# Indexer scores of the sample tokens by pairs in four column groups, earlier stores of the chunk inputs, weight tiles between small products, top-k inside the chunks

## The reference

```python
def _indexer_scores(qi, wi, ki):                      # 8 index heads of 64
    logits = jnp.einsum('bthd,bsd->bths', qi, ki)
    return jnp.einsum('bths,bth->bts', jax.nn.relu(logits), wi)
...
# prompt: 256 keys per query, the 64 largest are kept; sample: 1024 + 4 keys, the 256 largest are kept
...
def step(S, inp):                                      # mixer B, 16 heads, state 64 x 64
    r_t, dec_t, k_t, v_t, a_t, b_t = inp
    sa = jnp.einsum('bhij,bhj->bhi', S, a_t)
    S = S * dec_t[:, :, None, :] + sa[..., None] * b_t[:, :, None, :] + v_t[..., None] * k_t[:, :, None, :]
    return S, jnp.einsum('bhij,bhj->bhi', S, r_t)
```

## Time and profile before

| | |
|---|---|
| median of 3 runs | 2201.64 us |
| the profiled execution | 2200.62 us |
| its span | 2198.8 us |
| TensorE busy | 2071.0 us, 94% |
| VectorE busy | 1053.5 us, 48% |
| ScalarE busy | 748.1 us, 34% |
| mean granted TensorE clock | 0.957 of full |

### The profile page before, as it was taken

How to read it: one execution, slowest core, us unless ns; L and a number is a source line. 1 busy time by engine, 2 the same in 40 slices (tenths; PEclk the granted TensorE clock), 3 DMA queues, 4 the chain that set the end, 5 groups by cost and what they waited for, 6 DMA issues and landing times.

```text
span 2198.8 us, 38331 instructions
## 1 busy us (share of the span) xinstructions
PE 2071.0 (94%) x15658; PEld 1850.0 (84%) x15658; DVE 1053.5 (48%) x1262; ACT 748.1 (34%) x1005; POOL 39.6 (2%) x60
## 2 busy tenths in 40 slices
PE   5999966999998999998999899999999999899997
PEld 4999754658885765557999899999999999899997
DVE  4444865806765620114444455554545554343434
ACT  3333302352223210004444345444444444233332
POOL 0000002100000000000000000000000000000000
PEclk9999987899998998888999999999999999999998
DMA  5444344234542289992454555444444444454543
GB/s 190 161 159 165 109 157 133 65 98 133 172 144 87 77 312 359 378 372 95 165 172 155 186 193 166 170 170 156 169 171 158 168 172 158 162 170 159 169 159 122
DMA packets 97260, 375.76 MB, mean 171 GB/s; under 512 B 28003, under 2 KB 38883, under 8 KB 69795
## 3 DMA queue, kind: packets, MB, share of 16 engines
q1 hardware_dynamic: 71058, 335.36, 43.7%
q10 hardware_dynamic: 21152, 19.66, 2.8%
q0 software_dynamic: 4976, 19.71, 2.6%
HBM read 358.14 MB, written 16.53 MB: 170 GB/s over the span
## 4 chain that ended last, share of the span: by engine, by line
PE 85%; DVE 7%; DMA 3%; SPq 2%; ACT 2%; issue 1%; DVEq 0%; ACTq 0%; POOL 0%; POOLq 0%
PE ps L425 13%; PE ps L921 13%; PE ps L922 13%; PE ps L923 12%; PE ps L876 5%; PE ps L877 5%; PE ps L878 5%; PE ps L460 2%; PE ps L459 2%; PE ps L461 2%; PE ps L817 2%; PE ps L849 1%; DMA gram<-arena 1%; PE ps L861 1%; PE ps L581 1%
## 5 line engine op out<-in xcount | busy, mean ns | idle before, releaser
L1776 DVE TENSOR_TENSOR weights_lo<-ring,weights_hi 128x2048 fp32r<-128x2048 f32 (+1 forms) x152 | 305.6, 2011 | 294.1 <-ACT weights_hi L1330 284.1
L922 PE MATMUL ps<-h_lo,weights_hi 128*128 128x288 f32 x1408 | 416.2, 296 | 0.0
L921 PE MATMUL ps<-h_hi,weights_hi 128*128 128x288 f32 x1408 | 414.6, 294 | 0.3 <-DVE weights_lo L1776 0.3
L923 PE MATMUL ps<-h_hi,weights_lo 128*128 128x288 f32 x1408 | 412.5, 293 | 0.0
L1330 ACT ACTIVATE weights_hi<-ring 128x2048 fp32r<-128x2048 f32 (+1 forms) x152 | 257.1, 1691 | 374.8 <-PE ps L923 365.7
L425 PE MATMUL ps<-hT,ring 128*128 128x288 f32 x1472 | 380.4, 411 | 1.2 <-ACT arena L1107 1.2
L425 PEld LDWEIGHTS ps<-hT,ring 128*128 128x128 f32 x1472 | 273.3, 191 | 79.4 <-issue 7.0
L923 PEld LDWEIGHTS ps<-h_hi,weights_lo 128*128 128x128 f32 x1408 | 265.1, 188 | 0.0
L921 PEld LDWEIGHTS ps<-h_hi,weights_hi 128*128 128x128 f32 x1408 | 264.1, 188 | 0.5 <-DVE weights_lo L1776 0.5
L922 PEld LDWEIGHTS ps<-h_lo,weights_hi 128*128 128x128 f32 x1408 | 264.4, 188 | 0.1
L921 PE MATMUL ps<-act_hi,weights_hi 128*128 128x288 f32 x704 | 209.7, 298 | 6.1 <-DVE weights_lo L1776 4.2
(11 more groups left out here) (339 smaller groups left out, 3083.3 us busy)
## 6 DMA issues: line engine op xcount, KB each, us to landing
ring<-in_wst SPq DMA_DIRECT2D x201, 1024.0 KB, 4.9
ring<-in_wdn SPq DMA_DIRECT2D x64, 704.0 KB, 4.0
arena<-in_kT SPq DMA_DIRECT2D x64, 512.0 KB, 5.7
arena<-in_v SPq DMA_DIRECT2D x64, 512.0 KB, 5.9
ring<-in_wst ACTq DMA_DIRECT2D x8, 1024.0 KB, 8.0
arena<-chunk_ar_bk ACTq DMA_DIRECT2D x24, 256.0 KB, 3.7
arena<-in_ki SPq DMA_DIRECT2D x64, 64.0 KB, 1.8
chunk_ar_bk<-arena POOLq DMA_DIRECT2D x2, 2048.0 KB, 14.4
```

What stands on the lines that cost most here:

```text
L921: mm(out, W_HI[:, (u - U_FF) % 2, w], hi, start=start, stop=False)
L922: mm(out, W_HI[:, (u - U_FF) % 2, w], lo, start=False, stop=False)
L923: return mm(out, W_LO[:, u % 4, w], hi, start=False, stop=stop)
L1776: tt(W_LO[:, u % 4, 0:m], raw, W_HI[:, at, 0:m].bitcast(F32), ALU.subtract).then_inc(sem("w_split"), 1)
```

## The change

- `scores(pair)` takes two sequences: four products of 32 rows, for two sequences and two halves of the 1024 keys, to the four groups of 32 columns of one bank. ScalarE applies one relu to all of it. `scores_sum(pair)` is two products, one for each half of the keys, which add into two banks over the four pairs (`start=(pair == 0)`, `stop=(pair == 3)`) with weights `WSM` that hold zeros for the other sequences. The scores of the new tokens with themselves are a small group of their own in bank 7. The sum of 32 rows goes straight to `SCS`, so the stores and the load of `sample_scores` go.
- All queries are built at once (`QS`), and three key buffers of two sequences each take the place of two of one sequence.
- GpSimd stores `ARt` when it is done, `BKt` in two halves, and loads the states; SyncE stores the grams.
- One tile stands between two grams, two between rotary products, one after every second prompt score product, and one between the groups of the 128 state products.
- Eight of the 16 prompt score products, those of the second query tile, move behind `sample_step(9)`, and the last step between them. 141 tiles are done where the chunks begin, 137 before.
- The prompt top-k goes into the chunks, one turn at the end of each; the mask `MP` is made after the last.

The diff, cut to its core:

```diff
@@ SyncE
             ki_pages(0)
-            ki_pages(1)
-            units(8, U_VKQ + 8, unit)
-            for b in range(NB):
...
+            units(8, U_VKQ + 7, unit)
+            for c in range(NCH):
+                sp.wait_ge(sem("gram_out"), c + 1)
+                sp.dma_start(gram_d[c], GS[:, c % 2, :]).then_inc(sem(f"gram_stored{c % 2}"), 16)
+            ki_pages(1)
+            units(U_VKQ + 7, U_VKQ + 8, unit)
+            ki_pages(2)
+            units(U_VKQ + 8, U_VKQ + 9, unit)
+            sp.wait_ge(sem("sidx"), 1)
+            ki_pages(3)
@@ TensorE
+            def scores(pair):
+
+                pe.wait_ge(sem(f"ki_in{pair % 3}"), 16 * 2 * NPG * (pair // 3 + 1))
+                if pair:
+                    pe.wait_ge(sem("sidx_relu"), pair)
+                for n in range(4):
+                    half, a = n // 2, n % 2
+                    ins = mm(ps[2][32 * n:32 * n + 32, :], QS[:, 2 * pair + a, :],
+                             KIB[pair % 3][:, a, half * 512:(half + 1) * 512], start=True, stop=True)
+                ins.then_inc(sem("sidx"), 1)
+
+            def scores_sum(pair):
+
+                pe.wait_ge(sem("sidx_relu"), pair + 1)
                 for half in range(2):
+                    at = 64 * half
+                    ins = mm(ps[3 + half][0:NSAMP, :], WSM[at:at + 64, pair, :], RL[at:at + 64, :],
+                             start=(pair == 0), stop=(pair == 3), skip_group_check=True)
+                ins.then_inc(sem("sidx_sum"), 1)
...
+            fill(U_VKQ, 75, 78)
+            scores_sum(0)
+            sample_step(0, 78)
+            fill(U_VKQ, 86, 89)
+            scores(1)
...
+            fill(U_VKQ, 110, 115)
+            sample_step(6)
+            fill(U_VKQ, 115, 121)
+            sample_step(7)
+            fill(U_VKQ, 121, 127)
+            sample_step(8)
+            fill(U_VKQ, 127, 133)
+            sample_step(9)
+            pe.wait_ge(sem("scs_out"), 2)
+            for n in range(IH, 2 * IH):
+                prompt_scores(n)
+                fill(U_VKQ, 125 + n, 126 + n)
+                if n == IH + 5:
+                    sample_step(10)
+            at_tile = 141
@@ VectorE
-            with dve.Fori(0, TOPK_P // 8) as i:
...
+            def prompt_largest():
+
                 for qt in range(2):
-                    settle(dve)
                     ch(nc.vector.max(out=M8[:, qt, :], in_=SCP[:, qt, :]))
...
                 if n < 4:
                     update(n)
                 largest()
+                prompt_largest()
@@ GpSimd
-            for a, src in enumerate((ARt, BKt)):
-                pool.dma_start(arbk_d[a].rearrange("c p n -> p c n"),
-                               src.rearrange("p c j n -> p c (j n)")).then_inc(sem("arbk_stored"), 16)
+            pool.dma_start(arbk_d[0].rearrange("c p n -> p c n"),
+                           ARt.rearrange("p c j n -> p c (j n)")).then_inc(sem("ar_stored"), 16)
+            for part, n in ((slice(0, 4), 4), (slice(4, 8), 5)):
+                pool.wait_ge(sem("dve_stage"), n)
+                pool.dma_start(arbk_d[1][part].rearrange("c p n -> p c n"),
+                               BKt[:, part].rearrange("p c j n -> p c (j n)")).then_inc(sem("bk_stored"), 16)
             pool.dma_start(SST, wkv_d).then_inc(sem("states_in"), 16)
-            for c in range(NCH):
-                pool.wait_ge(sem("gram_out"), c + 1)
-                pool.dma_start(gram_d[c], GS[:, c % 2, :]).then_inc(sem(f"gram_stored{c % 2}"), 16)
```

More of the change, by code:

```diff
@@ L103, in constants @@
     put("negblk", np.concatenate([future, other], 1))
-    put("spread", np.repeat(np.eye(IH), NS, axis=1))
+    put("spread", np.tile(np.repeat(np.eye(IH), NS, axis=1), (1, 4)))
+    row, own = np.arange(P), np.arange(NSAMP)
+    put("wmask", np.concatenate([(own[None, :] // NS == 2 * n + (row[:, None] // NSAMP) % 2)
+                                 & (own[None, :] % NS == row[:, None] % NS) for n in range(4)], 1).astype(np.float32))
     put("dmask", (tt[:, None] == tt[None, :]).astype(np.float32))
@@ L558, in scores_sum @@
-            def scores_sum(b):
-                pe.wait_ge(sem("sidx_relu"), 3 * (b + 1))
-                for half in range(2):
-                    mm(ps[2 + half][0:NS, :], WSB[0:NSAMP, b % 2, :], RL[0:NSAMP, half * 512:(half + 1) * 512],
-                       start=True, stop=True)
-                mm(ps[4][0:NS, 8:8 + NS], WSB[0:NSAMP, b % 2, :], RL[0:NSAMP, PAST:PAST + NS],
-                   start=True, stop=True).then_inc(sem("sidx_sum"), 1)
-            def sample_step(n):
+            for n in range(IH):
+                prompt_scores(n)
+                if n % 2 == 1:
+                    fill(U_VKQ, 69 + n // 2, 70 + n // 2)
@@ new lines, in _ @@
+            act.wait_ge(sem("self"), 1)
+            fn(RLS[0:64].rearrange("p n t -> p (n t)"), ps[7][0:64, 0:4 * NS], ACT.Relu).then_inc(sem("self_relu"), 1)
+            scores_relu(0)
+            act.wait_ge(sem("self"), 2)
+            fn(SCS[0:NSAMP, PAST:], ps[7][0:NSAMP, 16:16 + NS], ACT.Copy).then_inc(sem("self_relu"), 1)
+            for par in range(2):
+                act.wait_ge(sem(f"gram_stored{par}"), 16 * NCH // 2)
+            act.wait_ge(sem("ar_stored"), 16)
+            stage_b(0)
@@ new lines, in _ @@
+            stage_a(0)
+            evict(86)
+            sample_step(0)
+            scores_relu(1)
+            evict(92)
+            sample_step(1)
+            scores_relu(2)
+            evict(98)
+            sample_step(2)
+            evict(102)
+            sample_step(3)
+            evict(106)
+            sample_step(4)
+            scores_relu(3)
+            evict(110)
+            act.wait_ge(sem("sidx_sum"), 4)
+            for half in range(2):
+                fn(SCS[0:NSAMP, half * 512:(half + 1) * 512], ps[3 + half][0:NSAMP, :], ACT.Copy).then_inc(
+                    sem("scs_out"), 1)
@@ new lines, in _ @@
+            sample_step(5)
+            evict(115)
+            sample_step(6)
+            evict(121)
+            sample_step(7)
+            evict(127)
+            sample_step(8)
+            evict(133)
+            sample_step(9)
+            for n in range(IH, 2 * IH):
+                prompt_relu(n)
+                evict(126 + n)
+                if n == IH + 5:
+                    sample_step(10)
+            at_tile = 141
+            act.wait_ge(sem("inv_stored"), 32 * NCH)
+            stage_inverse(0)
@@ L1548, in _ @@
                     sem("pidx_sum"), 1)
[L1550 removed]
+            for n in range(IH):
+                prompt_sum(n)
             dve.wait_ge(sem("gl_in"), 32 * NCH)
```

253 lines of the change are left out of this document (115 added, 138 removed).

## The result

The changed kernel took 2182.9 us (median of 5 runs, 2181.13 to 2189.44) against 2201.64 us (5 runs): ratio 0.9925, 95% interval 0.9903 to 0.9948. The forecast was 2163 us with a range of 2146 to 2177 us, so the sign was right and the gain half of what was said. The profiled execution took 2181.13 us, its span is 2179.0 us, 19.8 us less than before.

The account below looks back on a forecast made before the run. TensorE's own path bounds the kernel, with idle time and halved clock ahead of the chunks. A to G sum to 151.8 us against 194.3, 42.5 less; minus 4.8 at the tail, 2200.6 becomes 2163 us, range 2146 to 2177.

Parts of the forecast that it names:

- A: The first 52 value projection tiles, from 291.17 us: 25.4 us, with `BKt` ending while they run.
- C: Rotary products with eight tiles in the gaps of VectorE's chain: 9.6 us.
- D: Eight prompt score products and four single tiles: 7.9 us, including 1.7 us for a possible low clock.
- E: Self scores, first pair's `scores(0)` and `scores_sum(0)`, with tiles and waits between: 6.2 us.
- rival 2: Gram waits stay at 8 us instead of 1.5, or column and row groups don't overlap; both give 2182 us; 15%.
- B: Nine grams and nine single tiles, stores on SyncE's queue nearly hidden: 16.5 us, including 1.5 us of waits.
- F: `sample_step(0)`: transposes, state products and eight single tiles, mostly at the low clock: 29.5 us.
- rival 1: Clock holds through the state products and prompt scores: 13 us less, 2150 us; 25%.
- G: The rest up to the first chunk tile, at the high clock: 56.7 us.
- rival 4: TensorE never returns to the high clock before the chunks: slower, 2235 us; 3%.
- Rival 3: VectorE becomes the bound of the chunks, each losing up to 2.3 us to the top-k: 2181 us; 5%.
- The tail: Behind the last chunk: top-k turn adds 2.3 us of wait, transposes at the low clock 2.5 us; 4.8 us lost.

Follow-up runs that it names:

- the run with 96: Changed kernel plus 96 instructions (waits met at once) at the head of TensorE's program; 2177.68 us, ratio 0.9891 to the kernel before.
- states_late: the run with 96, with GpSimd's load of the 2 MB of states moved behind its wait for the gram stores; 2170.11 us, ratio 0.9856.
- gs4_late: states_late with four buffers instead of two for the grams on their way to memory; 2171.7 us, ratio 0.9854.
- all_three: states_late with four gram buffers and the eight tiles put behind the 256 state products; 2163.53 us, ratio 0.9821.
- all_four: all_three with the last chunk's top-k turn put behind the two last rotary evictions; 2155.48 us, ratio 0.9792.
- turn_behind: states_late with the last chunk's top-k turn put behind VectorE's two last rotary evictions; 2170.31 us, ratio 0.9844.

## Why the prediction was half right

By its own steps, in the profiled executions; 37.7 us were forecast and 19.8 us came.

- **A, C, D, E:** 25.3, 9.4, 6.8 and 5.5 us against 25.4, 9.6, 7.9 and 6.2. Right within 1.1 us. `scores(0)` took 1.0 us (0.9), `scores_sum(0)` 1.0 us (1.3): column and row groups overlap, and rival 2 falls in its second half. That its "both 2182 us" is the measured time is luck: the pairs did not fail, and other terms filled the sum.
- **B, the grams:** 25.7 us against 16.5, and over the 23.0 us of the upper bound that the waits were given (the same code took 22.2 us in the run with 96). The step that failed is "the stores now have SyncE's queue (...) so it nearly hides". A queue of its own did not take the first store out of the traffic of the 4 MB that GpSimd had issued at 311.19, 316.05 and 316.79 us. I had priced the round trip by a later wait (2.06 us) and by a median over eight stores (2.4 us), and such a median hides the first ones. The sign set for it, no DMA wait of over 4 us, failed with 7.25 us. The trace after shows 2.0 us in the median for the eight, while the first three took 8.9 us, beside the states' 15.5:

```profile
arena<-in_wkv POOLq DMA_DIRECT2D x1, 2048.0 KB, 15.5
gram<-arena SPq DMA_DIRECT2D x8, 256.0 KB, 2.0
```

That rival 2 named the mechanism, with 15%, and its bound of 8 us, helps little: states_late shows that it was the main case, and the kernel after that a low clock behind the waits can come on top. With four buffers as well, which hide most of what is left, the grams take 15.8 us (gs4_late, all_three and all_four alike), near the 16.5 that I had summed with 1.5 us of waits.

- **F:** 32.2 us against 29.5. The fall of the clock was taken rightly (at 370 us), so rival 1 falls. The size of the cutting was off: at the low clock 32 instructions of the products take 3.11 us from start to start and a tile 1.26 us, where I had 2.62 and 1.15. The Trainium skill (TensorEngine Tiling (Array Packing), "Instruction Overhead") gives a matmul about 60 cycles, and I had read the rows as nearly twice that. A record of the trace is two instructions by the count above, so the 256 records are 512 instructions: 12.8 us by that figure at 2.4 GHz, an estimate, against 11.8 us by the rows, so the two are near each other.
- **G:** 58.1 us against 56.7, part of it at 0.5 behind F. The clock of the whole rest stays at 1.00, so rival 4 falls.
- **The chunks:** TensorE never waits in them, and the slack of VectorE ahead of the first eviction in chunk 1 fell from 4.86 us to 2.88 us. Rival 3 falls.
- **The tail:** 4.8 us forecast, 1.1 us came, from the first chunk tile to the start of the paged attention. The idle time is 6.62 us, as said, and four tiles are missing. The 2.5 us for transposes that would start low were wrong: 16 instructions had taken 2.98 us before too, against 1.94 us at full clock in turn_behind, so they ran low in large part already (granted clock 0.59 over these 4.1 us), and the 2.98 us stood in the earlier trace rows.
- **"a gain here moves all later stages, which the change leaves as they are":** the second step that failed, and the largest error, 9.6 us of the paged attention, ahead of B's 9.2 us. I had listed a paged attention that gets longer as what would make the forecast wrong, but for its start in time, and that was not the cause. The place of the loop in TensorE's program was, by 51 instructions. The rows to ask were there: the count of instruction packets, and the lack of any in the second turn.

Together: 30.4 us at the chunks (with 0.9 us of a later start), less 1.1, less 9.6, is 19.7 us.

## What to carry to other kernels

When a change alters the number of instructions ahead of a loop on TensorE, look at the loop's jump back and at the count of instruction packets: an "issue" wait of several us there is a matter of place, and a few instructions ahead of the loop, where the engine waits anyway, repair it. A small store that the next step waits for needs not only a queue of its own but a time at which nothing large is in flight; move the large load that nobody needs yet. Ask also what the median over several transfers hides: the first of them can be the one that is waited for. And judge an edit by the trace up to the point behind it, not by the end alone: what gs4_late and turn_behind gained was there and was lost 35 us later to the clock. One profile does not say whether such a loss belongs to the kernel, since executions of one kernel differ by as much.

## What was not expected of the hardware

- A loop of 1577 instructions on TensorE turns back without a fetch when it begins at 0.56, 0.86, 0.95 or 0.125 of a packet of 256 instructions, and with nine packets fetched and 8.1 to 9.0 us of idle time when it begins at 0.75; this beside DMA engines that are 0.9 to 1.0 busy with key and value pages.
- Waits that are met at once are not free in numbers: 205 instructions of them moved the first product by 8.7 us, 256 by 14.2 us, while 96 moved it by 0.4 us, hidden behind the wait for its input (15.24 us against 14.85).
- The same prompt attention, 30 us of it, ran at a mean granted clock of 0.83 to 0.85 in the profiles of eight kernels and at 0.67 to 0.69 in those of six, and at nothing between, with nearly the same order of work. From its first product to the start of the paged attention it is 108.8 to 109.3 us in the eight and 113.6 to 116.0 us in the six, a difference by which executions of one kernel differ too. What the engine does ahead of it (idle for 2.3 or for 6.6 us) does not sort the two groups.
